# Attention branch slab as four transfers over all partitions, ahead of a modulation slab whose product moves behind W10

## The reference

```python
mod = einsum('bd,de->be', silu(c), ada_w) + ada_b          # 6 x 1024 columns
shift1, scale1, gate1, shift2, scale2, gate2 = split(mod, 6)
h = rms_norm(x, norm_mix_w) * (1.0 + scale1) + shift1
proj = einsum('bsd,de->bse', h, w_in)                      # q, k, v, the gated scan's inputs, gate logits
...
ya = einsum('bsw,wd->bsd', o_att, w_branch_att)            # 512 x 1024
yh = einsum('bsw,wd->bsd', o_hg, w_branch_hg)              # 512 x 1024
g = sigmoid(gate_logits)
merged = g[:, :, 0] * ya + g[:, :, 1] * yh
x = x + gate1 * (merged @ w_out)
```

## Time and profile before

| | |
|---|---|
| three runs | 1831.63, 1835.19, 1840.62 us; median 1835.19 |
| the profiled execution | 1830.55 us, of which the span of its instructions is 1828.4 us |
| busy over the span | PE 1473.4 us (81%), DVE 582.6 (32%), ACT 466.8 (26%), POOL 91.9 (5%) |
| granted PE clock, mean | 0.887 of full speed |
| DMA | 565.31 MB, mean 309 GB/s; queue q1 has 555.81 MB of it |

### The profile page before, as it was taken

The page is one execution under the profiler, slowest core; times in us unless marked ns, Lnnn a source line. Parts: engine busy times, 40 slices in busy tenths (PEclk is TensorE's granted clock), DMA queues, the critical chain, the costliest instruction groups (busy, mean ns, idle before and its releaser), DMA issues.

```text
span 1828.4 us, 21009 instructions
## 1 busy us (share of the span) xinstructions
PE 1473.4 (81%) x8891; PEld 927.3 (51%) x8891; DVE 582.6 (32%) x747; ACT 466.8 (26%) x660; POOL 91.9 (5%) x79
## 2 busy tenths in 40 slices
PE   3999988876667766777667766769899999989998
PEld 1987565322213222122212221228799978868997
DVE  3488364000000000000000000027655555755553
ACT  3676232000000000000000000025554444664442
POOL 2591000000000000000000000000000000000000
PEclk9999998988877778777787878789999999999999
DMA  9536779999999999999999999995455536425550
GB/s 353 170 117 229 220 298 366 429 427 429 428 428 428 429 428 428 428 429 429 427 430 428 429 428 429 428 387 184 152 193 188 190 141 208 150 103 185 184 184 24
DMA packets 97876, 565.31 MB, mean 309 GB/s; under 512 B 4780, under 2 KB 6072, under 8 KB 73240
## 3 DMA queue, kind: packets, MB, share of 16 engines
q1 hardware_dynamic: 95080, 555.81, 75.3%
q0 software_dynamic: 2112, 7.06, 1.2%
q10 hardware_dynamic: 624, 1.57, 0.2%
HBM read 563.37 MB, written 1.05 MB: 309 GB/s over the span
## 4 chain that ended last, share of the span: by engine, by line
DMA 45%; PE 42%; DVE 6%; ACT 4%; issue 3%; POOL 1%; SPq 0%; DVEq 0%; ACTq 0%; POOLq 0%
DMA ring_b<-in_w_exp_down_dram 22%; DMA ring_b<-in_w_exp_up_dram 21%; PE PS L2038 10%; PE PS L2039 10%; PE PS L2040 10%; PE PS L2369 3%; PE PS L2393 3%; DVE parts L1280 2%; PE PS L2021 1%; DMA ring_a<-in_w_branch_att_dram 1%; DMA arena<-in_ada_w_dram 1%; PE PS L2121 1%; ACT parts L791 1%; DVE rounded L1280 1%; ACT junk L809 1%
## 5 line engine op out<-in xcount | busy, mean ns | idle before, releaser
L1280 DVE TENSOR_TENSOR parts<-ring_a,parts 128x2048 fp32r<-128x2048 f32 (+1 forms) x101 | 235.7, 2337 | 159.0 <-ACT parts L791 158.6
L2369 PE MATMUL PS<-ring_a,arena 128*32 128x512 f32 x1232 | 177.7, 708 | 100.7 <-DMA ring_a<-in_w_exp_up_dram 61.2
L791 ACT ACTIVATE parts<-ring_a 128x2048 fp32r<-128x2048 f32 (+1 forms) x101 | 191.1, 1899 | 174.9 <-PE PS L2040 158.5
L2369 PE MATMUL PS<-ring_b,arena 128*32 128x512 f32 x768 | 134.7, 838 | 100.2 <-DMA ring_b<-in_w_exp_up_dram 61.6
L1689 DVE TENSOR_TENSOR arena<-PS,arena 128x512 f32<-128x512 f32 x16 | 11.1, 692 | 564.5 <-PE PS L2369 564.5
L2369 PEld LDWEIGHTS PS<-ring_a,arena 128*32 128x32 f32 x1232 | 36.4, 120 | 236.8 <-DMA ring_a<-in_w_exp_up_dram 102.5
L1016 ACT ACTIVATE arena<-PS 128x512 f32<-128x512 f32 x16 | 9.6, 597 | 564.0 <-PE PS L2369 564.0
L2038 PE MATMUL PS<-parts,hT 128*128 128x512 f32 (+1 forms) x352 | 130.1, 370 | 12.3 <-DVE parts L1280 4.3
L2393 PE MATMUL PS<-ring_b,arena 128*32 128x512 f32 x720 | 102.2, 701 | 44.6 <-DMA ring_b<-in_w_exp_down_dram 44.6
L2038 PE MATMUL PS<-hT,parts 128*128 128x256 f32 x448 | 127.8, 285 | 9.8 <-POOL hT L674 9.8
L2369 PEld LDWEIGHTS PS<-ring_b,arena 128*32 128x32 f32 x768 | 24.7, 133 | 205.3 <-DMA ring_b<-in_w_exp_up_dram 103.0
(11 more groups left out here) (329 smaller groups left out, 2176.6 us busy)
## 6 DMA issues: line engine op xcount, KB each, us to landing
ring_a<-in_w_exp_gate_dram SPq DMA_DIRECT2D x45, 2048.0 KB, 25.6
ring_b<-in_w_exp_down_dram SPq DMA_DIRECT2D x45, 2048.0 KB, 26.0
ring_a<-in_w_exp_up_dram SPq DMA_DIRECT2D x32, 2048.0 KB, 25.2
ring_b<-in_w_exp_up_dram SPq DMA_DIRECT2D x32, 2048.0 KB, 26.6
ring_a<-in_w_exp_down_dram SPq DMA_DIRECT2D x16, 2048.0 KB, 27.1
ring_b<-in_w_exp_gate_dram SPq DMA_DIRECT2D x16, 2048.0 KB, 23.4
ring_a<-in_w_up_dram SPq DMA_DIRECT2D x16, 2048.0 KB, 7.8
ring_a<-in_w_down_dram SPq DMA_DIRECT2D x16, 2048.0 KB, 7.6
```

What stands on the lines that cost most here:

```text
L791: act.activation(part_of(c, 0), raw(c), ACT.Copy).then_inc(chunk_high, 1)
L1280: dve.tensor_tensor(part_of(c, 1), raw(c), part_of(c, 0).bitcast(F32), ALU.subtract)\
L2369: ins = mm(PS[32 * j:32 * j + 32, side, :], xe[:, 2 * q + kk, :], w[:, kk, j * NB:(j + 1) * NB], start=q == 0 and kk == 0, stop=q == 3 and ...
```

## The change

- In `FIRST_SLABS`, `att` moves ahead of `ada5`; the order is now W10, ada4, att, ada5, hg, out0. So `att` lies in the ring place that `ada5` had and waits for the product of ada9, and `ada5` lies in the place that `att` had and waits for the chunks of W10. The place of `out0` is now freed by the chunks of `att`, that of `ada10` by the product of ada5.
- `att` is four transfers, one for each i, of 128 partitions by one row of 1024 floats. The source of each is a pattern with three dimensions, slowest first: 2 (step 262144 floats), 64 (step 1024), 1024 (step 1). The semaphore's count goes up by 64 for it, not 32.
- PE makes `ada_part(5)` behind the whole of W10, ahead of `ya0`, and `ada_row(5)` between `ya0` and `ya1`. `ada_row(4)` stays between the halves of W10. DVE's list follows, and the table of PSUM banks too.

```diff
-    + [("ada4", 1, 3), ("adc9", 1, 0), ("W10", 2, 3), ("ada5", 1, 0), ("adr4", 1, 2), ("adr5", 1, 0)]
-    + [("ya0", 2, 1), ("ya1", 2, 0), ("yh0", 2, 2), ("yh1", 2, 3)]
+    + [("ada4", 1, 3), ("adc9", 1, 0), ("W10", 2, 3), ("adr4", 1, 2), ("ada5", 1, 0)]
+    + [("ya0", 2, 1), ("adr5", 1, 2), ("ya1", 2, 0), ("yh0", 2, 2), ("yh1", 2, 3)]
...
-    + [(n, n) for n in ("W9", "ada8", "ada9", "W10", "ada4", "ada5")] + [("att", "ya1"), ("hg", "yh1")]
+    + [(n, n) for n in ("W9", "ada8", "ada9", "W10", "ada4")] + [("att", "ya1"), ("ada5", "ada5"), ("hg", "yh1")]
...
-    _count[_s] += 32 if _n == SLAB_AT["att"] else 16
+    _count[_s] += 64 if _n == SLAB_AT["att"] else 16
...
-                    for g in range(2):
-                        src = A["w_branch_att"][0, g * 256:(g + 1) * 256, :].rearrange("(i d) n -> d i n", d=AHD)
-                        load(n, src, dst=kn(n, 4)[64 * g:64 * g + 64])
+                    v = A["w_branch_att"][0]
+                    for i in range(4):
+                        src = bass.AP(tensor=v.tensor, offset=v.offset + i * AHD * D, ap=[[256 * D, 2], [D, AHD], [1, D]])
+                        load(n, src, dst=kn(n, 4)[:, i, :])
...
             split_to(CHUNK_OF["ya0"])
-            ada_part(5)
             dve.wait_ge(bias1_in, 32)
             ada_row(4, gate1[:, 0:NB])
             split_to(CHUNK_OF["ya1"])
-            ada_row(5, gate1[:, NB:D])
+            ada_part(5)
             split_to(CHUNK_OF["yh0"])
...
+                if n == 0:
+                    ada_row(5, gate1[:, NB:D])
                 split_to(CHUNK_OF["yh1"] + n)
...
-            natural("W10", hT, lambda: (ada_part(5), ada_row(4)))
+            natural("W10", hT, lambda: ada_row(4))
+            ada_part(5)
+            pe.wait_ge(oatt_low, 1)
+            branch("ya0", oattR)
             ada_row(5)
-            pe.wait_ge(oatt_low, 1)
-            for n in range(2):
-                branch(f"ya{n}", oattR)
+            branch("ya1", oattR)
```

## The result

The changed kernel takes 1862.9 us (median of 4 runs, 1862.3 to 1867.1) against 1833.9 us for the kernel before on the same chip (4 runs, 1831.6 to 1840.6): ratio 1.0152, 95% interval 1.0134 to 1.0171. By the medians it is slower by 29.0 us. The ratio is taken over all runs and is not the quotient of the two medians (1.0158); it makes 27.9 us, and its interval leaves 25 to 31 us. The forecast was 1863.0 us. The profiled execution of the changed kernel took 1863.37 us for a span of 1861.3 us.

The account below looks back on a forecast made before the run. No one engine bounds the whole (chain 45% DMA, 42% PE); a shift before the DMA-bound expert stream reaches the end one for one. 1830.55 + 27.8 = 1858.4 us profiled; at the median's level 1863.0 us, range 1855 to 1872.

Parts of the forecast that it names:

- Issue: `att` issued after ada9's product, at 207.33 instead of 207.75 us: gain 0.4 us; three of four issues hidden.
- Data: Two engines carry `att`'s 2.10 MB at 25.2 GB/s each: 41.6 us, plus 2.7 around it, landing at 251.6.
- ada5's slab: Queued behind `att`; 14 engines do their share at once, two need 5.3 us more; lands at 256.9.
- PE's wait: Behind W10, ending at 223.3, PE waits for ada5's slab until 257.0: 33.7 us.
- Restart: Clock down after the wait: ada5's product takes 3.64 us, to 260.6; about three slow `ya0` passes cost 0.6 us.
- `ya0` to `yh1`: 96 passes, 22.5 us, plus 0.85 us for ada5's row; `yh1` ends at 284.6 instead of 256.8: +27.8 us.
- Others: `hg`, `out0`, ada10 and the moved DVE copies and additions stay hidden or fall into idle time: cost 0.
- The signs that were named: DMA share near 0.13 at 215 to 245 us, `att` landing above 40 us, PE idle over 30, later chain shifted.
- full spread: Rival: `att`'s transfers use all 16 engines, PE never waits; 8.1 us less, 1827.1 us; chance 0.08.
- break-even: Within the full spread: `att`'s data through in some 13.5 us, 155 GB/s or six engines at 25.2; fewer is slower.
- eight engines: Rival: each `att` transfer gets another two engines; PE waits 2.7 us; 5.4 us less, 1829.8 us; chance 0.03.
- Two engines at half rate: Rival: each engine held to 13.5 GB/s, `att` lands 36.1 us later; +63.9 us, 1899 us; chance 0.04.

Follow-up runs that it names:

- 8 blocks: Changed kernel, but the source of each of the four `att` transfers cut into 8 blocks of 16 rows (slowest dimension 8): 1840.83 us, ratio 1.0038.
- 16 blocks of 8 rows: Changed kernel, but the source of each of the four `att` transfers has slowest dimension 16 instead of 2: 1827.40 us, ratio 0.9958.
- 4 blocks: Changed kernel, but the source of each of the four `att` transfers cut into 4 blocks of 32 rows (slowest dimension 4): 1850.56 us, ratio 1.0084.

## Why the prediction was right

The mechanism is shown, each link of it by a run: two engines for a slowest dimension of 2 (share 0.13, and 0.26, 0.55, 1.05 for 4, 8, 16), the same two each time, and the order not the cause (0.9978 without the four transfers, 1.0191 without the new order). That 1863.0 met 1862.9 to a tenth is luck: the shift was forecast 1.2 us too small (27.8 against 29.0 by the medians), and the level it was added to, 1835.19, lay 1.3 us above the median of before with its fourth run. The profiled execution itself took 5.0 us more than the 1858.4 forecast for it. By steps:

1. *Issue.* Predicted 207.3, was 206.69; this profile lies 0.7 us earlier. But "three of four issues are hidden behind the data, about 1 us each" was wrong in kind: the four took 19.27 us on SP, the next one 9.72, the one behind 12.55. No time was lost by it that shows here: the two engines had rows to move all the while, and their data ended last.
2. *Data.* 41.6 us with 2.7 around it predicted 251.6; the split began at 253.93, 2.3 us late, and 2.9 counted from the issue. The rate was right while `att` was alone (52 GB/s against 50.4); what was missing is the crowding. The second transfer, alone, took 9.9 us, the third 10.8 and the fourth 12.9, when ada5's slab ran beside them (250 GB/s at a share of 0.94 at 240 to 245 us) and then `hg`'s (325 GB/s at 1.01 at 250 to 255 us).
3. *ada5's slab.* 256.9 predicted, PE started on it at 259.04: the same 2 us, and 5.1 us behind `att` as worked out (5.3). The 14 engines did not do their share at once, as the sum had it: SP's issue was held until 235.72, and they moved it from 236.4 to 244.9 us, still ahead of the two.
4. *PE's wait.* 33.7 predicted, 36.45 measured; W10's last pass began at 222.20, where the sum implies 223.0; 0.7 us of that is how much earlier this profile lies.
5. *Restart.* 3.64 predicted, 3.54 measured. The 0.6 us of slow passes did not come: `ya0`'s first passes took 0.50 and 0.40 us, as with the clock up, and 262 to 264 us shows a granted clock of 0.91. The clock came back some 3 us after the restart, not 5.
6. *`ya0` to `yh1`.* 22.5 + 0.85 + 0.6 predicted; from 262.51 to 286.04 it was 23.5: 22.7 for the passes and 0.86 for the row.
7. *Others.* `hg` was split at 263.95 and hidden, as predicted; so was `out0`.

Sum: +27.8 predicted, +29.3 at `yh1`'s end. Inside the stretch, which leaves out how early the profile lies, 77.3 us were predicted (284.6 - 207.3) and 79.5 measured: 2.9 too few for the data, 0.6 too many for slow passes, the rest 0.2 or less each. The signs that were named came too, down to the shift at the first expert slab (32.7 us), which is found again at the end of the span (32.9); only the share of 0.13 did not last to 245 us. The further step, that the shift reaches the end one for one, holds by the medians (29.0) and by the table (+30.0 in the stretch against 27.9, interval 25 to 31).

The rivals. The *full spread* was priced at -8.1 us for 400 GB/s; given such a rate by another layout the kernel gains 8.2 us in the stretch and 8.3 by the ratio, so the price was right and only the condition false. Its break-even was not: "six engines at 25.2, 155 GB/s" would be enough. Eight engines were still 7 us slower, since the step took engines to work side by side unhindered. The same holds for *eight engines*, priced at 1829.8: its case, another pair for each transfer, never arose, and the nearest run, 8 blocks on eight engines, took 1840.83. *Two engines at half rate* is excluded by 26 GB/s for each.

The second rule cited in the prediction, that of the Trainium skill, "SBUF — State Buffer", section "Door 1: The DMA port swizzle", with half the ports for 64 partitions and all for 128, agrees with the rates of whole slabs (211 against 407 GB/s) but did not come to bear, because two engines limited the transfer first. And 128 partitions are not enough: 16 blocks of 8 rows had 16 engines, 128 partitions and 245 GB/s. The Trainium skill, "DMA: Bandwidth & Descriptors", section "The descriptor swizzle", says that in a plain transfer to 128 partitions each engine keeps to the partitions of one port, four here and four 32 higher; if 16 blocks of 8 rows give each engine eight neighbouring partitions instead, every port has two engines, and when all write the lower four of their eight at once, half of the ports stand idle. That fits 245 GB/s; no row shows which partitions an engine wrote, and blocks that lie 128 KB apart in the source are a rival that no run tested, so it stays an explanation that was argued.

## What to carry to other kernels

Before a source pattern is written by hand, read its slowest dimension: for 2, 4, 8 and 16 it was the number of DMA engines that carried the transfer. From the first issue to the first split 2 MB took 47.2 us on two engines, 29.9 on four and 22.6 on eight (with what ran beside them), against 13.1 in two halves of 64 partitions and 7.5 to 7.9 over 128. The pattern with 128 partitions as the slowest dimension on both sides is the one that reached 400 GB/s here; if the data doesn't have it, it can be worth laying out the operand on the chip otherwise so that the weight does, which here turned +29 us into -8 us. A narrow transfer harms what stands behind it twice, by the queue order and by crowding, so price it together with its followers.

## What was not expected of the hardware

- **Issues stall behind a narrow transfer.** SP's issues took 0.4 to 1 us each before, and 2.8 to 12.5 us behind transfers on two engines (in the changed kernel 8.2 and 9.8 us for the third and fourth of `att` already); with 4 blocks 5.04 and 13.89 us for the two slabs behind, with 8 blocks 0.47 and 10.74. Whatever else SP has to issue waits too, though 14 engines are idle.
- **Two deals crowd each other.** 8 blocks and a plain slab together moved 197 GB/s with all 16 engines busy; one after the other 158 and then 377 (4 us stretches of one profile each; the ratios of 1.0038 and 1.0011 bear it out).
- **The granted clock in the expert part varies from profile to profile, whatever the kernel.** The product of 64 passes that took 8.38 us before, at a granted clock of 0.84, and 9.91 after, at 0.71, took 8.4 us in 5 of the 13 profiles and 9.5 to 10.0 in the other 8; the 5 hold both the kernel that was slowest and one of the fastest. What decides it no run shows. Most of the 3.4 us that the profile of the changed kernel shows beyond 29.3 are of this kind, and the medians don't have them.
